# Strassen's scheme for two of three column groups of the up projection

## The reference, cut to what matters

```python
hn = _rms(x, p['norm_mlp'])                                    # 1056 tokens x 1024
x = x + jnp.square(jax.nn.relu(hn @ p['w_up'])) @ p['w_down']  # 1024 -> 4096 -> 1024
```

## Time and profile before

| | |
|---|---|
| median of 3 runs | 2299.33 us |
| profiled execution | 2297.07 us |
| its span | 2295.3 us |
| granted TensorE clock, mean | 0.978 |
| TensorE busy | 2158.4 us (94%) |
| VectorE busy | 1137.0 us (50%) |
| ScalarE busy | 676.9 us (29%) |
| GpSimd busy | 174.0 us (8%) |
| HBM | 77 GB/s over the span |
| up projection (first to last matmul) | 1512.3 to 1888.0 us |
| down projection, first matmul | 1889.8 us |

### The profile page before, as it was taken

One profiled execution on the slowest core, in us unless ns is written; L12 is line 12 of the kernel. 1 busy time (PEld: TensorE's weight loads), 2 busy tenths in 40 slices (PEclk: granted clock), 3 DMA queues, 4 the chain that ended last, 5 costly groups with the idle time before them and its releaser, 6 DMA issues.

```text
span 2295.3 us, 34228 instructions
## 1 busy us (share of the span) xinstructions
PE 2158.4 (94%) x13609; PEld 2059.3 (90%) x13609; DVE 1137.0 (50%) x1895; ACT 676.9 (29%) x1104; POOL 174.0 (8%) x303
## 2 busy tenths in 40 slices
PE   4999998999999799999999688999999999999998
PEld 3988888899998799999998588999999999999997
DVE  6424432667675355455443476642222235556566
ACT  5232213223233333334342343010000013333343
POOL 1100011222221200000000111010000000000000
PEclk9989999999999899999999899999999999999999
DMA  4111233222221421111110555132111114111112
GB/s 175 43 50 60 69 55 134 88 72 71 75 71 46 134 60 56 49 46 49 46 54 20 175 184 196 46 132 93 55 46 46 46 65 169 46 46 38 45 47 94
DMA packets 85071, 177.38 MB, mean 77 GB/s; under 512 B 10672, under 2 KB 53632, under 8 KB 84752
## 3 DMA queue, kind: packets, MB, share of 16 engines
q1 hardware_dynamic: 75376, 144.89, 19.7%
q0 software_dynamic: 9600, 31.62, 3.9%
q10 hardware_dynamic: 32, 0.01, 0.0%
HBM read 128.86 MB, written 47.62 MB: 77 GB/s over the span
## 4 chain that ended last, share of the span: by engine, by line
PE 83%; DVE 6%; DMA 3%; ACT 3%; issue 3%; POOL 1%; DVEq 0%; SPq 0%; POOLq 0%; ACTq 0%
PE PS L497 22%; PE PS L498 21%; PE PS L499 21%; PE PS L1021 2%; PE PS L1147 2%; PE PS L1138 2%; PE PS L1152 2%; DMA RING<-in_w_all 1%; DMA AR<-zrows 1%; ACT AR L1552 1%; PE PS L1009 1%; DVE AR L2401 1%; PE PS L1199 1%; PE PS L1045 1%; PE PS L1185 1%
## 5 line engine op out<-in xcount | busy, mean ns | idle before, releaser
L497 PE MATMUL PS<-HT_parts,W_parts 128*128 128x358 f32 (+1 forms) x1440 | 508.8, 353 | 13.9 <-ACT AR L549 10.1
L498 PE MATMUL PS<-OT_parts,W_parts 128*128 128x358 f32 (+1 forms) x1440 | 475.9, 330 | 0.0
L499 PE MATMUL PS<-HT_parts,W_parts 128*128 128x358 f32 (+1 forms) x1440 | 474.6, 330 | 0.0
L497 PEld LDWEIGHTS PS<-HT_parts,W_parts 128*128 128x128 f32 x1440 | 277.3, 193 | 22.8 <-issue 10.1
L498 PEld LDWEIGHTS PS<-OT_parts,W_parts 128*128 128x128 f32 x1440 | 277.1, 192 | 1.8
L499 PEld LDWEIGHTS PS<-HT_parts,W_parts 128*128 128x128 f32 x1440 | 276.8, 192 | 0.0
L497 PE MATMUL PS<-HN_parts,CF_parts 128*128 128x352 f32 x768 | 249.1, 324 | 1.2 <-DVE OT_parts L581 1.2
L498 PE MATMUL PS<-OT_parts,CF_parts 128*128 128x352 f32 x768 | 248.6, 324 | 0.0
L497 PE MATMUL PS<-ACT_parts,CF_parts 128*128 128x352 f32 x720 | 236.2, 328 | 12.8 <-issue 7.1
L499 PE MATMUL PS<-HN_parts,RING_parts 128*128 128x352 f32 x768 | 248.0, 323 | 0.0
L499 PE MATMUL PS<-ACT_parts,RING_parts 128*128 128x352 f32 x720 | 232.0, 322 | 0.0
(11 more groups left out here) (401 smaller groups left out, 3647.2 us busy)
## 6 DMA issues: line engine op xcount, KB each, us to landing
RING<-in_w_all SPq DMA_DIRECT2D x132, 512.0 KB, 3.6
zrows<-AR SPq DMA_DIRECT2D x102, 179.0 KB, 1.9
AR<-zrows SPq DMA_DIRECT2D x32, 528.0 KB, 3.6
zrows<-AR SPq DMA_DIRECT2D x60, 176.0 KB, 1.9
AR<-zrows SPq DMA_DIRECT2D x8, 640.0 KB, 4.5
AR<-in_xT SPq DMA_DIRECT2D x8, 537.0 KB, 7.0
HT<-in_xT POOLq DMA_DIRECT2D x8, 528.0 KB, 6.7
residual<-HT POOLq DMA_DIRECT2D x8, 528.0 KB, 7.0
```

The source lines that it names most:

```text
L497: e.matmul(out, whi, xhi, start=first, stop=False)
L498: e.matmul(out, whi, xlo, start=False, stop=False)
L499: return e.matmul(out, wlo, xhi, start=False, stop=last)
```

## The change: what it does, and the diff

The 8 input tiles are taken as an upper and a lower half (tiles 0 to 3, 4 to 7), the output tiles as two (tile i and tile i + 16 of the 32), and for the column groups G0 and G1 the product of a 2 x 2 grid of weight blocks (A11, A12, A21, A22) with a 2 x 2 grid of activation blocks is made by the scheme of Strassen in Winograd's form: 7 block products instead of 8, with sums of weight blocks (S1 to S4) and of activation blocks (T1 to T4). G2 is multiplied in the plain way, 4 block products. A round makes two output tiles from these 11 "units" of 4 blocks each. Activation sums are built once, weight sums in every round. Products are put together by VectorE as they leave PSUM (UP1 to UP4 hold partial sums; ScalarE copies the first product to UP1).

Sums T1 to T4, S1 to S4 and their parts lie where `ACTA` was, so only the last four rounds (8 rows) stay in SBUF, in `HT`. The 24 rows of rounds 0 to 11 go through `STG` to DRAM, VectorE waits at the head of a round until both rows of the round before have landed, and POOL reads them back in three groups of eight when the last product has been read. SP loads the weights of round i when VectorE has made the last low part of round i - 1.

The diff is cut to its core. TensorE:

```diff
+            def up_round(i, first):
+                def unit(name, xh, xl, bank, start, stop):
+                    for k in range(4):
+                        last = split_mm(e, PS(bank, 0, LGRP), UH_R[name][:, k], UL_R[name][:, k], xh(k), xl(k),
+                                        start and k == 0, stop and k == 3)
+                    last.then_inc(S("up_unit"), 1)
...
+                ready("A11", 4)
...
+                unit("A11", *block(0, G0), 0, True, True)
...
+                unit("A11", *block(0, G2), 4, True, False)
+                ready("A21", 4)
+                unit("A21", *block(0, G2), 5, True, False)
+                ready("A12", 8)
+                unit("A12", *block(4, G2), 4, False, True)
+                ready("A22", 8)
+                unit("A22", *block(4, G2), 5, False, True)
+                if first:
+                    sq_pe(e, 1, RST2)
+                ready("S3", 9)
+                read(READS)
+                unit("S3", *added(T3), 3, True, True)
+                ready("S2", 10)
+                unit("S2", *added(T2), 1, True, True)
+                ready("S1", 11)
+                if first:
+                    e.wait_ge(S("rstd"), 2)
+                unit("S1", *added(T1), 2, True, True)
+                if first:
+                    e.wait_ge(S("hn_ready"), 12)
+                unit("A12", *block(4, G0), 6, True, True)
+                if first:
+                    e.wait_ge(S("hn_ready"), 13)
+                unit("A22", *added(T4), 7, True, True)
+                ready("S4", 14)
+                read(3, True)
+                unit("S4", *block(4, G1), 1, True, True)
```

VectorE, a round (`done(n)` waits for unit n, `lo` makes a low part and waits for ScalarE's high part):

```diff
+                done(4)
+                relu(m0[:, G2], bank(4), 2).then_inc(S("up_read"), 1)
+                done(5)
+                relu(m1[:, G2], bank(5), 2).then_inc(S("up_read"), 1)
+                e.wait_ge(S("up_first"), i + 1)
+                done(7)
+                e.tensor_tensor(UP2, bank(1), UP1, ALU.add).then_inc(S("up_read"), 1)
+                e.wait_ge(S("up_read"), RD + 3)
+                e.tensor_tensor(UP3, bank(3), UP2, ALU.add).then_inc(S("up_read"), 1)
+                e.wait_ge(S("up_read"), RD + 4)
+                if first:
+                    rest_of_operands()
+                done(8)
+                e.tensor_tensor(m1[:, G1], bank(2), UP3, ALU.add).then_inc(S("up_read"), 1)
+                e.tensor_tensor(UP4, bank(2), UP2, ALU.add).then_inc(S("up_read"), 1)
+                e.wait_ge(S("up_read"), RD + 5)
+                relu(m1[:, G1], m1[:, G1], 1)
+                if more:
+                    lo("A11")
+                    lo("A21")
+                    raw_sum(USUM["S3"], RAW["A11"], RAW["A21"], ALU.subtract)
+                    lo("S3")
+                    raw_sum(USUM["S1"], RAW["A21"], RAW["A22"], ALU.add)
+                    e.wait_ge(S("up_raw"), nr + 2)
+                    raw_sum(USUM["S2"], USUM["S1"], RAW["A11"], ALU.subtract)
+                    lo("S2")
+                    lo("S1")
+                done(9)
+                e.tensor_tensor(m0[:, G0], bank(6), UP1, ALU.add).then_inc(S("up_read"), 1)
+                e.wait_ge(S("up_read"), RD + 7)
+                relu(m0[:, G0], m0[:, G0], 0)
+                lo("A12")
+                done(10)
...
+                lo("A22")
+                done(11)
...
+                relu(m0[:, G1], m0[:, G1], 1).then_inc(S("banks_free0"), 1)
+                if more:
+                    e.wait_ge(S("up_raw"), nr + 3)
+                    raw_sum(USUM["S4"], RAW["A12"], USUM["S2"], ALU.subtract)
+                    lo("S4")
...
+            with e.Fori(1, ROUNDS - 4) as i:
+                e.wait_ge(S("act_spilled"), i * 32)
+                up_round(i, lambda i, u: STG[:, u], True)
```

VectorE, before the first round, after the last tile's residual (excerpt; `operand_lo` and `block_lo` make low parts):

```diff
+            residual(3, 1)
+            block_lo("A21", up_hi(0, "A21"))
+            operand(3, 1, False, 20)
+            for name in ("A12", "A22"):
+                block_lo(name, up_hi(0, name))
+            raw_sum(TL[T3], B22, B12, ALU.subtract)
+            norm_sum(3, 1)
+            raw_sum(USUM["S3"], RAW["A11"], RAW["A21"], ALU.subtract)
+            raw_sum(TL[T2], B22, TR1, ALU.subtract)
+            e.wait_ge(S("up_raw"), 3)
+            raw_sum(TL[T4], B21, TL[T2], ALU.subtract)
+            raw_sum(USUM["S1"], RAW["A21"], RAW["A22"], ALU.add)
+            block_lo("S3", up_hi(0, "S3"))
+            operand_lo(T3, TL[T3], 1)
...
+            operand_lo(T2, TL[T2], 2)
+            block_lo("S2", up_hi(0, "S2"))
+            block_lo("S1", up_hi(0, "S1"))
+            operand_lo(T1, TR1, 4)
...
+            block_lo("S4", up_hi(0, "S4"))
+            e.tensor_tensor(OT_R[:, 4:8, G0], B21, HNH_R[:, 4:8, G0].bitcast(F32), ALU.subtract).then_inc(S("hn_ready"), 1)
+            def rest_of_operands():
+                operand_lo(T4, TL[T4], 3)
+                e.tensor_tensor(OT_R[:, 4:8, G1], B22, HNH_R[:, 4:8, G1].bitcast(F32), ALU.subtract).then_inc(S("hn_ready"), 1)
```

ScalarE makes all high parts of weights and sums and the squares of a round; POOL and SP:

```diff
+                    free(2)
+                    block_hi("A11")
...
+                    free(6)
+                    sum_hi("S3", nr + 1)
+                    free(7)
+                    sum_hi("S2", nr + 3)
+                    sum_hi("S1", nr + 3)
+                    free(9)
+                    block_hi("A12")
+                    free(10)
+                    block_hi("A22")
+                for u in (1, 0):
                     e.wait_ge(S(f"banks_free{u}"), i + (EV_UP + 1))
+                    e.activation(y, y, ACT.Square).then_inc(S("act_sq"), 1)
+                if more:
+                    free(11)
+                    sum_hi("S4", nr + 4)
...
+            with e.Fori(0, ROUNDS - 4) as i:
+                for u in (1, 0):
+                    e.wait_ge(S("act_sq"), i * 2 + (2 - u))
+                    e.dma_start(late(ACTS[...]), late(STG[:, u])).then_inc(S("act_spilled"), 16)
...
+            for q in (8, 16, 24):
+                for r in range(q, q + 8):
+                    m = act_tile(r)
+                    e.dma_start(late(act_row(r)), late(ACTS[m if m < 16 else m - 4])).then_inc(S("act_back"), 16)
+                e.wait_ge(S("act_back"), 16 * q)
...
+            with e.Fori(1, ROUNDS) as i:
+                e.wait_ge(S("parts"), i * 8 + UP_PARTS)
+                up_load(i)
```

To have semaphores for this, some others are shared. One of these edits joins two waits in the branch stage:

```diff
-                e.dma_start(late(HT[:, r]), late(OS[r])).then_inc(S(f"o_back{i // 2}"), 16)
+                e.dma_start(late(HT[:, r]), late(OS[r])).then_inc(S(f"o_back{min(i // 2, 1)}"), 16)
...
-                if r in (0, 4, 6):
-                    e.wait_ge(S(f"o_back{r // 3}"), 32)
+                if r in (0, 4):
+                    e.wait_ge(S(f"o_back{r // 4}"), 32 + 8 * r)
```

More of the change, by code:

```diff
@@ L417, in build @@
         ALO_R = [CF_R[:, w0:w0 + W], ACT_R[:, 2 * W:3 * W]]
-        def act_row(r):
-            return ACTA[:, r] if r < 16 else HT[:, r - 16] if r < 24 else ACTB[:, r - 24]
-        SQ3 = Arena(0).take(u=2, t=W)
-        SQ3R = Arena(2 * W).take(t=W)
-        ENDH_R = [MIX_R[:, 3 + i] for i in range(5)] + [MIXH_R[:, i] for i in range(3)]
-        ENDL_R = [MIXH_R[:, 3 + i] for i in range(5)] + [HT_R[:, i] for i in range(3)]
+        G0, G1, G2 = (group(g, True) for g in range(3))
+        TN = 4 * LGRP
@@ new lines, in at_up @@
+        def at_up(x, o, n):
+            return x[:, o:o + n].rearrange("p (k c) -> p k c", k=4)
+        TH_R = [at_up(UP_R, 2 * i * TN, TN) for i in range(4)]
+        TL_R = [at_up(UP_R, (2 * i + 1) * TN, TN) for i in range(4)]
+        TL = [at_up(AR, (2 * i + 1) * TN, TN) for i in range(4)]
+        T1, T2, T3, T4 = range(4)
+        WS0 = 8 * TN
+        UH_R, UL_R = {"A11": WHI_R[:, 0, 0:4], "A21": WHI_R[:, 1, 0:4]}, {"A11": WHI_R[:, 0, 4:8], "A21": WHI_R[:, 1, 4:8]}
+        UH_R["A12"], UL_R["A12"] = RING_R[:, 1, 0:4], RING_R[:, 1, 4:8]
@@ new lines, in build @@
+        USUM = {}
+        for i, name in enumerate(("A22", "S1", "S2", "S3", "S4")):
+            o = WS0 + 8 * P * i
+            UH_R[name], UL_R[name], USUM[name] = at_up(UP_R, o, 4 * P), at_up(UP_R, o + 4 * P, 4 * P), at_up(AR, o + 4 * P, 4 * P)
+        USUM["S2"] = at_up(AR, WS0 + 40 * P, 4 * P)
+        assert WS0 + 44 * P <= 2 * KD * W
+        RAWA = CF[:, w0:w0 + KD * P].rearrange("p (k c) -> p k c", k=KD)
+        RAWB = RING[:, 0]
+        RAW = {"A11": RAWA[:, 0:4], "A12": RAWA[:, 4:8], "A21": RAWB[:, 0:4], "A22": RAWB[:, 4:8]}
@@ new lines, in build, with up_hi @@
+        TR1 = ACTB[:, 0:4, G1]
+        UP1, UP2, UP3, UP4 = (HN2[:, i, G1] for i in range(4))
+        ACTS = nc.dram_tensor("act_rows", (24, P, W), F32, kind="Internal").ap()
+        FIRST = ("A11", "A21", "A12", "A22", "S3", "S2", "S1", "S4")
+        LATER = ("A11", "A21", "S3", "S2", "S1", "A12", "A22", "S4")
+        UP_PARTS, UP_HI, UNITS, READS, ROUNDS = 20, 2 * 34, 11, 9, 16
+        def up_hi(i, name):
+            return UP_HI + 8 * i + ((FIRST if isinstance(i, int) and i == 0 else LATER).index(name) + 1)
@@ new lines, in up_parts, with act_tile @@
+        def up_parts(i, name):
```

(55 more changed lines are left out.)

280 lines of the change are left out of this document (178 added, 102 removed).

## The result

The changed kernel takes 2275.09 us (median of 4 runs, 2273.0 to 2278.83) where the kernel before took 2298.91 us (4 runs, 2298.31 to 2300.6): ratio 0.990, 95% interval 0.9887 to 0.9912. The forecast was 2278, with a range of 2269 to 2296. The profiled execution took 2273.0 us, span 2271.3, so 24.0 us less span than the one of before.

What follows compares the result with a forecast made beforehand. TensorE, busy 94% of the span, was taken as the bound. -31.0 + 10.0 - 1.6 + 0.5 + 0.9 = -21.2 us turned the profiled 2297.1 into 2275.9, predicted as 2278 for the median; range 2269 to 2296.

Steps and rivals of the forecast that it cites:

- Matmuls: Up projection: 2112 matmuls for 2304, at 0.1615 us a step, take 31.0 us less.
- Start: Up projection, rounds 0 and 1: TensorE waits 8.0 and 2.0 us for VectorE's operands; lost clock adds 0.5 us.
- Old wait: Start of the up projection: 1.6 us of TensorE's earlier wait and restart go away.
- The merged wait: Branch stage: waiting for four rows of the mixers' output together makes it 0.5 to 1.4 us later, taken as 0.9.
- Steady rounds: Up projection's middle rounds: TensorE sets 21.3 us a round; VectorE's list has 1.5 us to spare before A12.
- Rival (a): VectorE or the landing sets the middle rounds: up to 17 us more, 2279 to 2295, middle 2288; chance 0.22.
- Landing: Rows stored to DRAM, rounds 1 to 11: land in 3.0 to 4.0 us; some 6 us allowed before TensorE feels it.
- Rival (b): Slower: each wait in VectorE's loop body blocks the register work behind it; 2315 at 0.35 us a wait; chance 0.12.

Runs made afterwards that it cites:

- e1_twelve: The change with unit 9 multiplied twice in every round, so 144 matmuls a round again: 2304.81 us, ratio 1.0021 to the kernel before.
- e7_first12: The change with its first round done by 12 plain block products while T1 to T4 are built: 2267.12 us, ratio 0.9868 to the kernel before.
- e2_busy: The change with 16 more matmuls in round 0 behind the sum over the norm, result unused: 2276.0 us, ratio 0.989 to the kernel before.
- e4_oback: The change with the branch stage's merged wait for rows of the mixers' output undone: 2275.42 us, ratio 0.9884 to the kernel before.
- e5_chain3: The change with VectorE's sum S1 made four times instead of once in rounds that prepare weights: 2285.23 us, ratio 0.9947 to the kernel before.
- e9_land2: The change with each of the 24 rows stored twice and VectorE's wait counting both: 2300.23 us, ratio 1.0011 to the kernel before.
- e3_start: The change with five raw sums of round 0 moved to GpSimd and VectorE's and ScalarE's lists reordered: 2282.59 us, ratio 0.9916 to the kernel before.
- e6_chain6: The change with VectorE's sum S1 made seven times instead of once in rounds that prepare weights: 2328.43 us, ratio 1.014 to the kernel before.

## Why the prediction was right

It was right in place, sign and main mechanism, and within 3 us in size. Two of its smaller steps did not hold: how covers add, and which slack of a steady round is used up first.

- **Matmuls, -31.0:** confirmed by e1_twelve (28.9 and 2.1 taken back; a round longer by 12 steps). The step is still 0.1615 us; in steady rounds TensorE is without a gap.
- **Start, +10.0 and 0.5 for the clock; measured 8.2.** The place was right (unit 6 for T3 low: 3.5 forecast, 3.12 measured; VectorE's T3 low ends at 14.7 us for 15.1), and so was the cause, as e7_first12 shows. Oversized was the tail: 2.0 us in round 1 were 1.08. The clock fell as the row of before had suggested, filled the waits of units 7 to 9, and cost nothing (e2_busy, e4_oback).
- **Old wait, -1.6:** 1.5 by the same sum on the stage of before (375.5 - 2304 x 0.1615 - 1.9).
- **The merged wait, +0.9:** 0.97 at ScalarE, the output projection started 1.4 us later, but the up projection only 0.4: the stretch at half clock that the kernel before had at the head of the output projection (1417.8 to 1421.2, granted clock 0.50) was not there in the change (1.00 from 1418.4 to 1421.8). What the merge itself costs stays open (e4_oback).
- **Steady rounds bound by TensorE, slack 1.5 us:** forecast 21.3 us, measured 21.27. That the slack measured 1.46 and 1.47 is in part luck. The prediction took it from A12: it put 10.0 us from unit 8 to the end of A12's low part, where the trace has 9.5 (1688.10 to 1697.60), and the slack there is 1.64. What would set rounds 2 to 11 first is the loop through the store, with 1.48. Rival (a) was closer than its 0.22 sounds: 2 us more on VectorE's list (e5_chain3) made it true. Its 17 us were reckoned from the spare of A22; from A12's 1.5 they would be 20.
- **Landing:** 3.0 to 4.0 us forecast, 2.9 to 3.9 measured, and the 24 rows came back (median 7.2 us) before the down projection asked. But the step "a landing may take some 6 us before TensorE feels it" was wrong in its making: I had added covers that lie in series on one loop, and the 1.4 us by unit 8 were 0.84 (two additions lie before it). By e9_land2 the limit is 3.85 + 1.48 = 5.3 us from issue to release; that the sum did not suffer is due to the landing staying below 4. Rival (a)'s price for a landing of 7.2 us (13 us) was too low for the same reason: 1.9 us in 11 rounds are 21. Its 7.2 is also more than the third of the way that it names, which gives 6.5.
- **Rival (b)**, waits that block the register work: no trace of it. VectorE's operations follow each other at 0.43 to 0.61 us whether a satisfied wait lies between them or not, and at 0.72 where one needs the result of the one before (1692.60 to 1693.32 in the change).

## What to carry to other kernels

Where one engine is full and another has half its time free, a scheme that trades multiplications for additions pays by the count; what decides is the order of the additions in the first round and the slack of the loop. The slack is measured by lengthening the list rather than read off a gap, and one must then look at which wait has taken over. A warm-up is cured by giving the full engine work that needs nothing new, even more of it (12 units for 11), rather than by spreading the preparation over VectorE and GpSimd where they hold each other up, as in e3_start. Covers on the same loop do not add: only idleness inside the loop counts in every round, and of that only waits for something that does not move with the loop.

## What the runs showed of the hardware that I had not expected

Two-input operations of VectorE stood still while GpSimd added tensors in e3_start (3.42 us for 0.53). The clock's fall is not fixed by the length of a wait: after 3.1 us before unit 6 it fell in the change and stayed up in e1_twelve and e4_oback, whose instructions in the stage are the same up to there; in e6_chain6 it stayed up behind a wait of 2.54 us (1680.99), fell behind one of the same 2.54 (1804.11), and also fell behind one of 2.30 (1730.60).
